# All twelve pieces of a layer's modulation weights inside the mixer; the first expert's weight loads unrolled ahead of the expert loop

## The chip, the cores and the metric

The kernel runs on one core of one Trainium2 chip. The metric is the device time of one execution in microseconds (us), as the median of several runs.

## What is computed

Two blocks follow each other, all in float32, on 256 tokens of 1024 features. The first block has two layers of a hybrid mixer and a mixture of 16 experts; the second block has two layers that are modulated by a condition. Cut to what matters here:

```python
# first block, for each of 2 layers
proj = rms_norm(h) @ w_in[layer]            # nine parts of 512 columns: rq rk rv rg hq hf_fwd hf_bwd hi hg
...                                         # retention scan and HGRN2 scan, both directions
h = h + concat([r_out, h_out]) @ w_out[layer]
affinity = softmax(rms_norm(h) @ w_router[layer])
gate, idx = top_k(affinity.T, 32)           # each expert chooses 32 tokens
hid = silu(xe @ w_gate[layer, e]) * (xe @ w_up[layer, e])
h = h.at[idx].add((hid @ w_down[layer, e]) * gate)

# second block, for each of 2 layers
sh1, sc1, gt1, sh2, sc2, gt2 = split(silu(cond) @ w_ada[layer] + b_ada[layer], 6)   # for c and c_ctx
...                                         # pool mixer or attention, MLP; both use the six modulations
```

The modulation product `silu(cond) @ w_ada[layer]` (1024 x 6144 weights for each layer) depends on nothing of the first block. The kernel computes it in twelve pieces of 512 columns per layer, beside the first block.

## The kernel before, in words

**The ring.** All large weights go through `ring`, six slots of 2 MB in SBUF. SyncE (SP) issues every load in one program order; before a load it waits until the item that had the slot before has been used. The counter for this is `weights_used`, which TensorE raises once per item, in the order in which it uses them. So a load that waits holds back all loads behind it. In the mixer only slots 0 to 3 carry items, in turn; the room of slots 4 and 5 holds `w_high`, the rounded copies of two items. An item of the mixer is therefore issued when the item four places before it has been used. `items` and `free_at` (lines 281 to 297) hold the slot, the number and the wait of each item.

**The mixer.** `mixer_items()` (line 79) is the order, written by hand, in which TensorE uses the items of a layer: nine projections (RQ, RK, HFF, HFB, HQ, RV, HI, RG, HG) and, between them, pieces of `w_ada` (ADA). Behind them come the two halves of `w_out`. ScalarE (`high_item`, line 1090), VectorE and GpSimd (`low_item`, line 400) split each projection item in two halves into a rounded part (`w_high`) and the rest (`w_low`), since a product is done as three passes of reduced precision (`product`, lines 461 to 463). The split items numbered 5 and more (RV, HI, RG, HG and the two of `w_out`) get their low part from GpSimd. Which rounded copy ScalarE makes when is tied to places in the item list: the copy of the item three places ahead (`n + 3 in SPLIT`), and `w_out` 0 one place before the last projection. It stands in ScalarE's program between the copies of ADA rows, and waits for the item's landing.

**An ADA piece** is on TensorE 8 products with `silu(c)` (line 473) into bank 6, then on ScalarE a copy of the bank to `ada_rows` (through line 376, a helper that records every turn), then on TensorE 4 small products that turn the rows to columns (line 482) into bank 7, then on VectorE the addition of the bias into `mods`. The columns of one piece are done just ahead of the next piece's products.

**Units.** Between the projections of RV, HI, RG and HG, TensorE runs 16 units of the HGRN scan (line 619, the last two line 612), two after each half of a projection. VectorE prepares each unit (`kdec`, `qdec`, `hgrn_x`, `hgrn_f`) and merges it. VectorE's order follows the same item list: the bias of the piece before at each ADA, four units at each projection.

**Before the change** six pieces stand in the mixer and six, called late, behind `w_out`: one ahead of the router (line 728), one behind its logits (line 740), four behind the turned affinities (line 748). `late_columns` gathers the columns of the late ones in one bank and VectorE adds their bias once. Two of the late pieces use slots 4 and 5. Then SP waits for the second `w_out` item and enters the expert loop (line 2181), with six items for each expert: four of gate and up weights, two of down weights, 12 MB together.

**The expert loop.** For each expert TensorE gathers 32 tokens (line 778), multiplies by gate and up (line 791), turns, multiplies by down (line 809), and scatters (line 819). The items of expert e + 1 are issued as those of expert e are used.

Of the kernel before, what the change touches and what calls it, by code (L numbers as in the profile page):

```python
# [22 lines left out]
ALU = mybir.AluOpType  # L23
# [8 lines left out]
P = 128  # L32
D = 1024
KC = D // P
# [64 lines left out]
def build_program(nc, x, cols, w_in, w_out, w_router, w_gate, w_up, w_down, final_g, ctx_x, w_ada,  # L99
# [184 lines left out]
    for layer in range(DEPTH):  # L284
# [3 lines left out]
        slots += [order[n % 6] for n in range(len(ADA_LATE) + 6 * NEXP)]  # L288
        names = ([("mix", layer, n) for n in range(len(mixer_items()))]
                 + [("w_out", layer, n) for n in range(2)]  # L290
                 + [("late", layer, n) for n in ADA_LATE]
                 + [("moe", layer, e, n) for e in range(NEXP) for n in range(6)])
# [52 lines left out]
    def freed(eng, name):  # L345

        eng.wait_ge(*read_by[name])
# [76 lines left out]
    def _(pe):  # L424
# [64 lines left out]
        for l in range(DEPTH):  # L489
# [198 lines left out]
            late_bank = [None]  # L688

            def late_ada(n):  # L690

                if n == ADA_LATE[0]:
                    ada_columns(l, n - 1, ("ada_c", l, n - 1))
                else:
                    late_columns(n - 1)
                ada_item(l, ("late", l, n), n, ("ada", l, n))

            def late_columns(n):
                name = ("ada_c", l, "late")
                freed(pe, ("ada", l, n))  # L700
                if n == ADA_LATE[0]:
                    late_bank[0] = take(pe, name, 7)
                for j in range(4):
                    at_ = 8 * (n - ADA_EARLY) + 2 * j
                    ins = mm(late_bank[0][:, at_:at_ + 2], ada_s[:, j * P:(j + 1) * P], K("sel"),
                             start=True, stop=True)
                if n == ADA_LATE[-1]:
                    fill(ins, name)


# [17 lines left out]
            late_ada(ADA_LATE[0])  # L728
# [11 lines left out]
            late_ada(ADA_LATE[1])  # L740
# [6 lines left out]
            for n in ADA_LATE[2:]:  # L747
                late_ada(n)
            late_columns(ADA_LATE[-1])
# [294 lines left out]
    def _(act):  # L1044
# [79 lines left out]
        for l in range(DEPTH):  # L1124
# [102 lines left out]
            def ada_row(n):  # L1227
                name = ("ada", l, n)
                ps = full(act, name)
                free(f(ada_s[:, :], ps[:, :], ACT.Copy), name)  # L1230

# [3 lines left out]
            ada_row(ADA_LATE[0])  # L1235
# [11 lines left out]
            for n in ADA_LATE[1:]:  # L1247
                ada_row(n)
# [191 lines left out]
    def _(dve):  # L1440
# [80 lines left out]
        for l in range(DEPTH):  # L1521
# [181 lines left out]
            ada_bias(ADA_EARLY - 1)  # L1703
# [25 lines left out]
            for i, what in enumerate((topf, top)):  # L1729
# [3 lines left out]
            name = ("ada_c", l, "late")  # L1733
            ps = full(dve, name)
            n = 4 * len(ADA_LATE)
            free(tt(mods[:, l, 4 * ADA_EARLY:4 * ADA_ALL, :],
                    ps[:, 0:2 * n].rearrange("p (a b) -> p a b", b=2),
                    C("b_ada", NMOD * KC * l + 4 * ADA_EARLY, n).unsqueeze(2)
                    .broadcast_to([P, n, 2]), ALU.add), name)
# [405 lines left out]
    def _(sp):  # L2145
# [20 lines left out]
        for l in range(DEPTH):  # L2166
# [10 lines left out]
            for n in ADA_LATE:  # L2177
                load(("late", l, n), chunked(w_ada[l, :, n * 512:(n + 1) * 512]), eight)

            sp.wait_ge(weights_used, items[("w_out", l, 1)][1] + 1)  # L2180
            with sp.Fori(0, NEXP) as e:
                for n in range(6):
                    slot, number, _ = items[("moe", l, 0, n)]
                    sp.wait_ge(weights_used, 6 * e + (number - RING1 + 1))
                    if n < 4:
                        dst = ring[:, slot, :].rearrange("p (k a f) -> p k a f", k=2, a=2)
                        for a, w in enumerate((w_gate, w_up)):
                            src = w[l, bass.ds(e, 1), 2 * n * P:2 * (n + 1) * P, :]
# [129 lines left out]
```

## Time and profile before

| | us |
|---|---|
| median of 3 runs | 2313.32 |
| lowest, highest of the 3 runs | 2312.31, 2318.74 |
| span of the profiled execution | 2314.5 |
| TensorE busy in it | 1928.7 (83%) |
| VectorE busy | 816.0 (35%) |
| ScalarE busy | 605.9 (26%) |
| GpSimd busy | 170.2 (7%) |

The page gives no time of the profiled execution beside its span of 2314.5 us, which lies 1.2 us above the median. The span runs from the first to the last instruction of the slowest core. Shares of busy time are averages over stages with different limits, so the stages are read apart: mixer of layer 0 (to about 243 us), its router and first expert, its experts (to about 759 us), the same three for layer 1 (to about 1518 us), and the second block.

### The profile page before, as it was taken

Reading aid. Unit: us, or ns where it says so; the run is one execution under the profiler, and the core shown is the slowest. Engines: PE = TensorE matmul, PEld = TensorE weight load, DVE = VectorE, ACT = ScalarE, POOL = GpSimd, SP = SyncE. Lnnn points to the kernel's source line nnn. Section 1 sums busy time; section 2 is a strip of 40 time slices with the busy share of each in tenths; the row PEclk is TensorE's granted clock in tenths of the full one; section 3 lists DMA queues with packets and bytes.
Section 4 is the critical chain, followed back from the end, with each engine's and each line's share of the span. In section 5 each row is a group of like instructions: output and inputs, shape, how many; then the busy total and the mean of one; then the engine's idle time right before and its main releaser. Section 6 shows DMA issues by size and latency. Waiting matters only on the chain.

```text
span 2314.5 us, 26791 instructions
## 1 busy us (share of the span) xinstructions
PE 1928.7 (83%) x10580; PEld 1227.7 (53%) x10580; DVE 816.0 (35%) x1196; ACT 605.9 (26%) x850; POOL 170.2 (7%) x70
## 2 busy tenths in 40 slices
PE   6897887777777789788767777766999999987998
PEld 5876532222232587654222222235888887445887
DVE  6566200000000556630000000046454455564776
ACT  5523211101111452312111111135222122253433
POOL 1333000000000132300000000021000000010000
PEclk9998887777777799888788888888999999998999
DMA  7373999999999636389999999941322224302551
GB/s 265 110 254 112 345 375 410 410 410 410 409 410 410 229 136 219 145 309 382 410 410 409 410 410 409 410 185 37 109 74 107 108 73 148 116 27 106 184 182 55
DMA packets 184534, 585.99 MB, mean 253 GB/s; under 512 B 6688, under 2 KB 7840, under 8 KB 184224
## 3 DMA queue, kind: packets, MB, share of 16 engines
q1 hardware_dynamic: 183152, 579.89, 65.0%
q0 software_dynamic: 896, 3.67, 0.4%
q10 hardware_dynamic: 432, 1.70, 0.2%
q8 instruction: 35, 0.57, 0.1%
q14 instruction: 19, 0.16, 0.0%
HBM read 584.19 MB, written 1.05 MB: 253 GB/s over the span
## 4 chain that ended last, share of the span: by engine, by line
PE 56%; DMA 17%; SPq 13%; DVE 7%; ACT 5%; issue 2%; POOL 1%; DVEq 0%; ACTq 0%; POOLq 0%
DMA ring<-in_w_down 16%; SPq L2189 11%; PE bank L461 10%; PE bank L463 10%; PE bank L462 10%; PE bank L791 3%; PE bank L778 3%; PE bank L809 3%; PE bank L819 3%; PE bank L940 2%; PE bank L619 2%; PE bank L473 2%; SPq L2195 2%; PE bank L1031 1%; ACT w_high L376 1%
## 5 line engine op out<-in xcount | busy, mean ns | idle before, releaser
L791 PE MATMUL bank<-ring,xeT 128*32 128x512 f32 x2048 | 280.9, 698 | 77.8 <-DMA ring<-in_w_up 58.7
L809 PE MATMUL bank<-ring,hid_T 128*32 128x512 f32 x1024 | 201.5, 930 | 81.2 <-DMA ring<-in_w_down 69.6
L791 PEld LDWEIGHTS bank<-ring,xeT 128*32 128x32 f32 x2048 | 69.3, 121 | 250.2 <-issue 160.5
L461 PE MATMUL bank<-x_high,w_high 128*128 128x512 f32 (+1 forms) x512 | 174.7, 341 | 17.0 <-DVE x_low L376 12.0
L376 POOL TENSOR_TENSOR w_low<-ring,w_high 128x2048 fp32r<-128x2048 f32 x26 | 120.7, 4643 | 821.6 <-ACT w_high L376 819.8
L463 PE MATMUL bank<-x_high,w_low 128*128 128x512 f32 (+1 forms) x512 | 175.4, 343 | 0.0
L462 PE MATMUL bank<-x_low,w_high 128*128 128x512 f32 (+1 forms) x512 | 173.7, 339 | 0.0
L1842 DVE TENSOR_TENSOR w_low<-ring,w_high 128x1024 fp32r<-128x1024 f32 x128 | 152.9, 1232 | 36.0 <-ACT w_high L1298 32.7
L1298 ACT ACTIVATE w_high<-ring 128x1024 fp32r<-128x1024 f32 x128 | 127.3, 1050 | 142.6 <-DMA ring<-in_w_mlp_in 64.0
L461 PE MATMUL bank<-w_high,hid_high 128*128 128x512 f32 x384 | 150.4, 392 | 0.0
L462 PE MATMUL bank<-w_low,hid_high 128*128 128x512 f32 x384 | 150.4, 392 | 0.0
L463 PE MATMUL bank<-w_high,hid_low 128*128 128x512 f32 x384 | 150.3, 391 | 0.0
L809 PEld LDWEIGHTS bank<-ring,hid_T 128*32 128x32 f32 x1024 | 35.1, 143 | 209.7 <-DMA ring<-in_w_down 135.9
L819 PE MATMUL bank<-y_e,gate_T 128*128 128x512 f32 x256 | 117.5, 601 | 29.1 <-DVE y_e L1779 29.1
L1776 DVE TENSOR_TENSOR hid_e<-silu_g,bank 128x256 f32<-128x256 f32 x32 | 13.5, 421 | 362.2 <-ACT silu_g L1255 362.2
L1779 DVE COPY y_e<-bank 128x512 f32<-128x512 f32 x32 | 22.1, 692 | 306.8 <-PE bank L809 306.8
L461 PE MATMUL bank<-w_high,xs_high 128*128 128x512 f32 x256 | 108.5, 424 | 18.8 <-DVE xT_low L376 15.5
L778 PEld LDWEIGHTS bank<-onehot,xs 128*128 128x128 f32 x1024 | 123.5, 201 | 0.0
L778 PE MATMUL bank<-onehot,xs 128*128 x1024 | 123.5, 281 | 0.0
L461 PEld LDWEIGHTS bank<-x_high,w_high 128*128 128x128 f32 x512 | 97.3, 190 | 29.2 <-issue 17.6
L1255 ACT ACTIVATE silu_g<-bank 128x256 f32<-128x256 f32 x32 | 12.3, 384 | 380.1 <-PE bank L791 380.1
L819 PEld LDWEIGHTS bank<-y_e,gate_T 128*128 128x128 f32 x256 | 46.0, 189 | 122.2 <-ACT y_e L1260 76.3
(229 smaller groups left out, 2925.1 us busy)
## 6 DMA issues: line engine op xcount, KB each, us to landing
ring<-in_w_gate SPq DMA_DIRECT2D x128, 1024.0 KB, 18.5
ring<-in_w_up SPq DMA_DIRECT2D x128, 1024.0 KB, 18.6
ring<-in_w_down SPq DMA_DIRECT2D x64, 2048.0 KB, 22.4
ring<-in_w_ada SPq DMA_DIRECT2D x24, 2048.0 KB, 8.2
ring<-in_w_in SPq DMA_DIRECT2D x18, 2048.0 KB, 10.0
ring<-in_w_mlp_in SPq DMA_DIRECT2D x16, 2048.0 KB, 8.6
ring<-in_w_mlp_out SPq DMA_DIRECT2D x16, 2048.0 KB, 7.7
ring<-in_w_out SPq DMA_DIRECT2D x4, 2048.0 KB, 9.2
```

What stands on the lines that cost most here:

```text
L376: self.ins, self.mine = op(*args, **kw), "none"
L461: mm(ps, lh, rh, start=first, stop=False, skip_group_check=True)
L462: mm(ps, lh, rl, start=False, stop=False, skip_group_check=True)
L463: return mm(ps, ll, rh, start=False, stop=last, skip_group_check=True)
L473: ins = mm(ps[32 * g:32 * g + 32, :], cT[:, 2 * g + k, :], w[:, 2 * g + k, :], start=k == 0, stop=k == 1)
L778: ins = mm(psum[7][:, c * CAP:(c + 1) * CAP], xs[:, t, c * P:(c + 1) * P], onehot[:, t, bass.ds(e * CAP, CAP)], start=t == 0, stop=t == NT ...
L791: ins = mm(psum[4][32 * g:32 * g + 32, :], xeT[:, 2 * n + k, :], w[:, k, :, 256 * g:256 * (g + 1)], start=n == 0 and k == 0, stop=n == 3 a ...
L809: ins = mm(psum[5 + half][32 * g:32 * g + 32, :], hidT[:, n, 32 * g:32 * g + 32], w[:, g, half * 512:(half + 1) * 512], start=n == 0, stop ...
L819: ins = mm(psum[2 * half + t][:, :], GT[:, t * P:(t + 1) * P], Y[:, half * 512:(half + 1) * 512], start=False, stop=False, skip_group_chec ...
L1298: raw(w_high[:, n % 2, quarter(q)], ring[:, slot, quarter(q)], ACT.Copy).then_inc(S_("w_high_ready"), 1)
L1842: nc.vector.tensor_tensor(w_low[:, slot, quarter(q)], ring[:, slot, quarter(q)], w_high[:, n % 2, quarter(q)].bitcast(F32), ALU.subtract). ...
L2189: sp.dma_start(dst[:, :, a, :], src.rearrange("o (k p) f -> p (o k) f", p=P)).then_inc(landed[slot], 16)
```

## The change

Twelve ADA pieces stand in `mixer_items()`; the late pieces and all that belongs to them go. The loads of the first expert's six items are issued by `load`, each with the wait for its own slot, ahead of a loop over the experts 1 to 15.

```diff
 def mixer_items():
-    return [RQ, RK, HFF, HFB, HQ, RV, ADA, HI, ADA, ADA, RG, ADA, ADA, HG, ADA]
-ADA_EARLY, ADA_ALL = mixer_items().count(ADA), 12
-ADA_LATE = range(ADA_EARLY, ADA_ALL)
+    return [RQ, RK, HFF, HFB, HQ, RV, ADA, ADA, HI, ADA, ADA, ADA, ADA, RG, ADA, ADA, ADA, ADA,
+            HG, ADA, ADA]
+ADA_ALL = mixer_items().count(ADA)
...
-        slots += [order[n % 6] for n in range(len(ADA_LATE) + 6 * NEXP)]
+        slots += [order[n % 6] for n in range(6 * NEXP)]
...
-            if name == ("late", layer, ADA_EARLY):
+            if name == ("moe", layer, 0, 0):
                 count[2][4:6] = [count[0]] * 2
...
-            late_ada(ADA_LATE[0])
+            ada_columns(l, pending[0], ("ada_c", l, pending.pop()))
             transposes(("x2", l), lambda t: xs[:, t, :], xs_ready)
...
-            late_ada(ADA_LATE[1])
             pe.wait_ge(S_("affinity_ready"), NT * (l + 1))
...
-            for n in ADA_LATE[2:]:
-                late_ada(n)
-            late_columns(ADA_LATE[-1])
...
-            ada_row(ADA_LATE[0])
...
-            for n in ADA_LATE[1:]:
-                ada_row(n)
...
-            ada_bias(ADA_EARLY - 1)
+            ada_bias(ADA_ALL - 1)
...
-            for n in ADA_LATE:
-                load(("late", l, n), chunked(w_ada[l, :, n * 512:(n + 1) * 512]), eight)
-            sp.wait_ge(weights_used, items[("w_out", l, 1)][1] + 1)
-            with sp.Fori(0, NEXP) as e:
+            for n in range(6):
+                load(("moe", l, 0, n), expert_sources(slice(0, 1), n), expert_view(n))
+            with sp.Fori(1, NEXP) as e:
```

ScalarE, in the mixer of layer 0, from the copies of HI's product on. `ada_rows` is the copy of a piece's rows, `w_high` the rounded copy of an item (two halves), `ret_gate` the product of RG. Before:

```order
L376 ACTIVATE hgrn_v<-bank 128x512 [waits bank_free0,weights_used]
L376 ACTIVATE w_high<-ring 128x2048 [waits bank_free1,landed2,weights_used]
L376 ACTIVATE w_high<-ring 128x2048 [waits mix_high_ready]
L376 ACTIVATE ada_rows<-bank 128x512 [waits mix_high_ready,weights_used]
L376 ACTIVATE ada_rows<-bank 128x512 [waits bank_free6,weights_used]
L376 ACTIVATE ret_gate<-bank 128x512 [waits bank_free6,bank_full2]
```

and now:

```order
L376 ACTIVATE hgrn_v<-bank 128x512 [waits bank_free0,weights_used]
L376 ACTIVATE ada_rows<-bank 128x512 [waits bank_free1,weights_used]
L376 ACTIVATE ada_rows<-bank 128x512 [waits bank_free6,weights_used]
L376 ACTIVATE w_high<-ring 128x2048 [waits bank_free6,landed1,weights_used]
L376 ACTIVATE w_high<-ring 128x2048 [waits mix_high_ready]
L376 ACTIVATE ada_rows<-bank 128x512 [waits mix_high_ready,weights_used]
L376 ACTIVATE ada_rows<-bank 128x512 [waits bank_free6,weights_used]
L376 ACTIVATE ret_gate<-bank 128x512 [waits bank_free6,bank_full2]
```

The rounded copy of RG stood ahead of both rows of its stretch; it now stands between the second and the third of four.

SyncE, the loads of layer 0. Before:

```order
L2155 DMA ring<-in_w_ada 128x8x512 [waits weights_used]
L2155 DMA ring<-in_w_in 128x8x512 [waits weights_used]
L2155 DMA ring<-in_w_ada 128x8x512 [waits weights_used] x2
L2155 DMA ring<-in_w_in 128x8x512 [waits weights_used]
L2155 DMA ring<-in_w_out 128x8x512 [waits weights_used] x2
L2155 DMA ring<-in_w_ada 128x8x512 [waits weights_used] x6
L2181 UNCONDITIONAL_BRANCH [waits weights_used]
```

and now:

```order
L2113 DMA ring<-in_w_ada 128x8x512 [waits weights_used] x4
L2113 DMA ring<-in_w_in 128x8x512 [waits weights_used]
L2113 DMA ring<-in_w_ada 128x8x512 [waits weights_used] x2
L2113 DMA ring<-in_w_out 128x8x512 [waits weights_used] x2
L2113 DMA ring<-in_w_gate 128x2x1024 [waits weights_used]
L2113 DMA ring<-in_w_up 128x2x1024
L2113 DMA ring<-in_w_down 128x4x1024 [waits weights_used] x2
```

Four pieces stand ahead of RG and four ahead of HG in the queue, where one or two stood; the six behind `w_out` are gone, and the first expert's loads follow `w_out`, each with its own wait.

TensorE, from the last products of `w_out` to the router and the spread of the chosen indices, one piece of the difference:

```order
 L482 MATMUL bank<-consts_sb,ada_rows 128x2 x4
-L473 MATMUL bank<-ring,silu_c 32x512 x8
 L437 MATMUL bank<-consts_sb,xs 128x128 x16
-L737 MATMUL bank<-router_sb,xT 128x16 x16
-L705 MATMUL bank<-consts_sb,ada_rows 128x2 x4
-L473 MATMUL bank<-ring,silu_c 32x512 x8
-L745 MATMUL bank<-consts_sb,affinity 16x128 x2
-L705 MATMUL bank<-consts_sb,ada_rows 128x2 x4
-L473 MATMUL bank<-ring,silu_c 32x512 x8
```

Nothing of the pieces but the columns of the last one is left on TensorE behind `w_out`; the other lines of this piece come back in the changed kernel under new line numbers, without L705 and L473 between them.

## Rows read from the trace of the kernel before

**Rows 1.** Busy time by stretch, all engines: us, busy of each, PEclk, DMA share, GB/s.
```profile
0.00:243.00 243.00, 199.91 (x1194) 169.52 (x1195) 144.33 (x163) 94.87 (x113) 66.89 (x25) 0.92 0.51 182
243.00:291.00 48.00, 39.30 (x245) 26.19 (x243) 16.25 (x44) 11.89 (x21) 0.00 (x0) 0.79 1.03 399
295.10:758.60 463.50, 360.01 (x2170) 135.02 (x2165) 26.46 (x61) 65.50 (x92) 0.00 (x0) 0.79 1.02 408
```
**Rows 2.** The chain that ended last, layer 0's experts, layer 1's last: start, us, what.
```profile
306.12 22.31 DMA ring<-in_w_down
...
1493.91 23.60 DMA ring<-in_w_down
```
**Rows 3.** Timeline of TensorE, mixer of layer 0: start, us, engine, line, operation.
```profile
139.83 1.92 PE L473 MATMUL bank<-ring,silu_c 128*32 128x512 f32 x16
142.47 1.05 PE L482 MATMUL bank<-consts_sb,ada_rows 128*128 128x2 f32 x8 [0.72 <-ACT ada_rows L376]
143.45 1.92 PE L473 MATMUL bank<-ring,silu_c 128*32 128x512 f32 x16
...
213.83 2.40 PE L437 MATMUL bank<-consts_sb,xs 128*128 128x128 f32 x10 [4.56 <-DVE mods L376]
...
242.88 0.95 PE L482 MATMUL bank<-consts_sb,ada_rows 128*128 128x2 f32 x8
```
**Rows 4.** SyncE, RG's load (issued at 120.6 us) and HG's (145.4), time to landing.
```profile
DMA to landing us min/median/max: 9.0/9.0/9.0
...
DMA to landing us min/median/max: 10.3/10.3/10.3
```
**Rows 5.** Timeline of ScalarE, mixer of layer 0.
```profile
136.28 3.85 ACT L376 ACTIVATE w_high<-ring 128x2048 fp32r<-128x2048 f32 x2
...
175.06 3.86 ACT L376 ACTIVATE w_high<-ring 128x2048 fp32r<-128x2048 f32 x2 [4.15 <-DMA ring<-in_w_out]
```
**Rows 6.** TensorE at the lower clock: its timeline, and one stretch (us, busy, PEclk, DMA, GB/s).
```profile
189.72 2.08 PE L612 MATMUL bank<-qdec,kdec 128*128 128x128 f32 x8 [4.47 <-DVE qdec L376]
...
256.20 1.85 PE L705 MATMUL bank<-consts_sb,ada_rows 128*128 128x2 f32 x8
257.98 3.32 PE L473 MATMUL bank<-ring,silu_c 128*32 128x512 f32 x16
...
190.00:194.00 4.00, 3.79 (x17) 0.50 0.63 241
```
**Rows 7.** Timeline of GpSimd, mixer of layer 0.
```profile
177.05 9.79 POOL L376 TENSOR_TENSOR w_low<-ring,w_high 128x2048 fp32r<-128x2048 f32 x2 [4.66 <-ACT w_high L376]
207.71 9.44 POOL L376 TENSOR_TENSOR w_low<-ring,w_high 128x2048 fp32r<-128x2048 f32 x2 [20.88 <-ACT w_high L376]
```
**Rows 8.** Timeline of VectorE, mixer of layer 0.
```profile
176.74 0.69 DVE L376 TENSOR_TENSOR qdec<-hgrn_q,hgrn_f 128x512 f32<-128x512 f32 x1
177.46 4.94 DVE L376 TENSOR_TENSOR hgrn_x<-hgrn_x,hgrn_f 128x512 f32<-128x512 f32 x1
...
208.45 4.33 DVE L376 TENSOR_TENSOR ret_gate<-ret_gate,ret_stat 128x512 f32<-128x512 f32 x1
...
217.06 1.49 DVE L376 TENSOR_TENSOR xT_low<-xT,xs_high 128x512 fp32r<-128x512 f32 x2
...
226.21 0.69 DVE L376 TENSOR_TENSOR h<-h,bank 128x512 f32<-128x512 f32 x1 [3.99 <-PE bank L463]
```
**Rows 9.** Timeline, TensorE and VectorE, router of layer 0 to the spread of the indices.
```profile
258.73 0.50 DVE L376 TENSOR_SCALAR affinity<-logit,router_stat 128x16 f32<-128x16 f32 x2
...
261.23 0.39 PE L745 MATMUL bank<-consts_sb,affinity 128*16 128x128 f32 x2
...
267.78 0.68 DVE L376 TENSOR_TENSOR spread<-top_index_f,consts_sb 16x512 f32<-16x512 f32 x1
...
278.39 1.98 PE L761 MATMUL bank<-spread,ones 16*128 16x512 f32 x4
...
281.22 1.41 DVE L376 TENSOR_TENSOR gated<-onehot,bank 128x512 f32<-128x512 f32 x2
```

More of the change, by code:

```diff
@@ L287, in build_program @@
         order = [order[(len(slots) + n) % 4] for n in range(4)] + [4, 5]
-        slots += [order[n % 6] for n in range(len(ADA_LATE) + 6 * NEXP)]
+        slots += [order[n % 6] for n in range(6 * NEXP)]
         names = ([("mix", layer, n) for n in range(len(mixer_items()))]
                  + [("w_out", layer, n) for n in range(2)]
-                 + [("late", layer, n) for n in ADA_LATE]
                  + [("moe", layer, e, n) for e in range(NEXP) for n in range(6)])
         for name, slot in zip(names, slots):
-            if name == ("late", layer, ADA_EARLY):
+            if name == ("moe", layer, 0, 0):
                 count[2][4:6] = [count[0]] * 2
@@ L686, in _ @@
                     hgrn_out()
[L688 to L708, printed above, removed]
             def mix_ready(t):
@@ L1225, in out_ready @@
                     freed(act, ("w_out", l, n, t))
[L1227 to L1230, printed above, removed]
             for t in range(NT):
@@ L1731, in _ @@
                    delta, ALU.mult).then_inc(S_("spread_ready"), 1)
[L1733 to L1739, printed above, removed]
             if l == DEPTH - 1:
@@ L2176, in _, with expert_sources, expert_view @@
                 load(("w_out", l, n), chunked(w_out[l, :, n * 512:(n + 1) * 512]), eight)
-            for n in ADA_LATE:
-                load(("late", l, n), chunked(w_ada[l, :, n * 512:(n + 1) * 512]), eight)
-            sp.wait_ge(weights_used, items[("w_out", l, 1)][1] + 1)
-            with sp.Fori(0, NEXP) as e:
+            def expert_sources(e, n):
+                if n < 4:
+                    return [w[l, e, 2 * n * P:2 * (n + 1) * P, :].rearrange(
+                        "o (k p) f -> p (o k) f", p=P) for w in (w_gate, w_up)]
+                return [w_down[l, e, :, :].rearrange("o (g two p) d -> two p (o g) d",
+                                                     two=2, p=P)[n - 4]]
+            def expert_view(n):
+                if n < 4:
+                    return lambda s_: [s_.rearrange("p (k a f) -> p k a f", k=2, a=2)[:, :, a, :]
+                                       for a in range(2)]
+                return four
+            for n in range(6):
+                load(("moe", l, 0, n), expert_sources(slice(0, 1), n), expert_view(n))
+            with sp.Fori(1, NEXP) as e:
                 for n in range(6):
@@ L2184, in _ @@
                     sp.wait_ge(weights_used, 6 * e + (number - RING1 + 1))
[L2185 to L2188, printed above, removed]
-                            sp.dma_start(dst[:, :, a, :],
-                                         src.rearrange("o (k p) f -> p (o k) f", p=P)).then_inc(
-                                landed[slot], 16)
-                    else:
-                        src = w_down[l, bass.ds(e, 1), :, :].rearrange(
-                            "o (g two p) d -> two p (o g) d", two=2, p=P)[n - 4]
-                        sp.dma_start(ring[:, slot, :].rearrange("p (g d) -> p g d", g=4),
-                                     src).then_inc(landed[slot], 16)
+                    for out_, src in zip(expert_view(n)(ring[:, slot, :]),
+                                         expert_sources(bass.ds(e, 1), n)):
+                        sp.dma_start(out_, src).then_inc(landed[slot], 16)
         for l in range(DEPTH):
```

1 line of the change is left out of this document (added).

## The prediction

> **What bounds the kernel now.** I first cut the span into stages, since the page's shares average over them. From 295.1 to 758.6 us the DMA engines are full, at 408 GB/s [rows 1]; the chain of waits says the same, with a wait for a down-projection load of 22 to 24 us in every expert [rows 2]. Fifteen experts of 12 MB (12.58 million bytes) are 188.7 MB, and 463.5 us at 408 GB/s carry 189.1 MB. So this stage is a stream of fixed length. It starts when TensorE uses the first item of expert 0, because only then does a slot come free for expert 1. Whatever lands earlier than that gains nothing; whatever delays that moment delays the end one for one. The same holds for layer 1, whose last expert ends on such a load too [rows 2]. The second block is untouched. The question is therefore only how much earlier or later TensorE reaches expert 0 in each layer.
>
> That path has two parts. In the mixer (0 to 243 us) TensorE is busy 199.91 of 243 us and the DMA engines 0.51 [rows 1], so the mixer has DMA to spare but little TensorE. Behind it, from 243 to 291 us, DMA is full (1.03) and TensorE is busy 39.3 of 48 us [rows 1], partly with the late pieces. It looks tempting to move work from the second to the first. But the pieces take TensorE time wherever they stand, and in the second stage a part of them lies beside VectorE's search for the best tokens.
>
> **The gain behind the mixer.** The affinities are ready at 258.73 + 0.50 = 259.2 us; TensorE turns them at 261.23, since it is still in a late piece [rows 9]. That is 2.0 us, and with 0.3 to 0.4 us from the piece ahead of the router 2.3. VectorE then writes the first spread tensor until 268.46 us (267.78 + 0.68), and TensorE reads it only at 278.39, behind four late pieces and their columns [rows 9]. After the change it starts at 268.46 - 2.3 = 266.2. Those two products take 1.98 us; TensorE will have idled before them, so I take the lower clock, at which the small columns took 1.85 for 1.05 us and the products of a piece 3.32 for 1.92 us [rows 3, 6]: about 4.0 us. The gated tensor, at 281.22 before [rows 9], then starts at 270.3: **10.9 us earlier**. Bounds: 9 us, if something of VectorE's comes between, and 12.2 us at the full clock. The missing bias addition of the late pieces costs nothing either way; it lay under the same wait.
>
> The unrolled loads of expert 0 count as **zero**. They are issued as their slots come free and all have landed some 20 us after the last of w_out is used (six items take 31 us at 408 GB/s, and four of them, 20 us, come after w_out), while TensorE needs about 37 us from there to expert 0. Before, too, they did not hold it up. If that cover were gone, the cost could be some 5 us; a gain is excluded, as only the use of the first item frees a slot.
>
> **The cost in the mixer, layer 0; layer 1 is the same.**
>
> *a. TensorE's time.* Two pieces back to back are 3.62 us apart (139.83 to 143.45): columns 1.05, products 1.92, and a wait for ScalarE's copy [rows 3]. Five of the six added pieces stand between projections, where TensorE is nearly always busy: one before HI, two before RG, two before HG. 5 x 3.62 = **18.1 us**.
>
> *b. RG arrives late.* An item is issued when the item four places before it has been used. For RG this was the piece before HI, so a whole projection with four units lay between; now it is the first of the four pieces just ahead of RG. This piece ends where the second of two ended before, at 143.45 + 1.92 = 145.4 us [rows 3]. RG is issued there. A weight load behind another landed after 9.0 or 10.3 us, in the bounds of 8 to 10.3 [rows 4]; I take 9.0, as the load before it is 6 us ahead: 154.4. ScalarE's two rounded halves take 3.85 us [rows 5]: 158.2. As the order shows, ScalarE's copy of the third piece's rows is queued behind them: 158.8. The fourth piece needs that copy at 142.47 + 3 x 3.62 = 153.3. TensorE waits **5.5 us**. ScalarE can be held like this: before w_out's copy it stood 4.15 us for a landing [rows 5]. After a gap of 4.47 us TensorE ran at 1.2 GHz, granted clock 0.50 [rows 6]; so the fourth piece costs 1.85 + 3.32 = 5.17 for 2.97 us, **2.2 us** more. GpSimd's low halves (9.3 to 9.8 us [rows 7]) then just end in time. Together 7.7 us; bounds 4.5 (landing in 8 us, full clock) and 13 (10.3 us, and RG's first 24 products at the lower clock too).
>
> The Trainium skill, "DMA: Bandwidth & Descriptors", sections Specifications and Bandwidth, gives 0.6 us to the first byte and 425 GB/s for a large transfer, which would be an estimated 5.5 us for 2 MB. By that the wait would be 3.5 us shorter, twice in a layer, and the kernel's time 14 us less. The trace has 9.0 us for the same thing, and the trace decides.
>
> *c. HG arrives late*, by the same distances: **7.7 us**.
>
> *d. The last units.* VectorE operations with both inputs in SBUF take 0.69 us, but 4.94 while GpSimd makes its two low halves in 9.79 us [rows 7, 8]: such an operation waits for the end of a half, about 4.9 us. The wait is moved later with w_out 0, by about as much as the units are; I take -1 us, bounds -3 and +4.
>
> *e. The last piece* stands behind the scans, where TensorE idles. Its columns need the bank that VectorE frees with the bias of the piece before, queued behind VectorE's last write of xs (213.5 us). This write comes 3.6 us sooner, as GpSimd no longer works beside it (4.33 against 0.69 us [rows 8]): columns from 210.1, piece ended 215.3 at the lower clock, then all 16 transposes, 218.0. Before, they ended at 213.83 + 2.40 = 216.2 [rows 3]: **+1.8 us**.
>
> *f. w_out 1 is split late.* ScalarE makes its rounded copy after the rows of the last piece: 215.9 to 219.8, with ScalarE's own share of the xT chunks behind it. GpSimd's low halves then run from 217.9 to about 227.3, under VectorE's `xT_low`, which has two SBUF inputs and ran freely before (1.49 us for two, as GpSimd ended at 217.15 [rows 7, 8]). The first waits until 223.3, the second until 227.9, the third and fourth follow 2.1 us of chunks, at 230.7 and 231.4. The first w_out product, cut into four pieces by this and at the lower clock, ends at 235.9 instead of 226.2 [rows 8]: 9.7 us, of which 1.8 are in e. **+7.9 us**. Bounds: 0 if VectorE isn't held, 10.
>
> Sum: 18.1 + 7.7 + 7.7 - 1 + 1.8 + 7.9 = 42.2 us later at 242.88 us [rows 3], and 10.9 us back: **31.3 us for a layer, 62.6 for two**. The sum is made against the span of 2314.5; the median is 1.2 lower, and I take it as the base: 2313.3 + 62.6 = **2376 us**. With the bounds a layer loses 16 us (no lock, no clock lost) to 41 us: 2345 to 2395.
>
> **The rivals.**
>
> *The arrivals are covered.* The pieces cost only TensorE's time: 18.1 + 1.8 - 10.9 = 9 us a layer, **2331 us**. For it: ScalarE and DMA are slack on average. Against: the four-place distance, which the order shows.
>
> *The lower clock spreads.* With gaps of 5 us ahead of RG and HG the first 24 products of both go at 1.2 GHz (each about 4.6 us more), and landings take 10.3 us: 31.3 + 9.2 + 2.6 = 43 us a layer, **2400 us**.
>
> *Faster.* The mixer has DMA to spare, and gaps of TensorE for all six pieces. Then only the gain stays: 10.9, and the 3.6 us of VectorE in e, for a layer, **2284 us**. It decides for faster once the mixer grows by less than 10.9 us, that is if fewer than three of the five pieces show. For it: the mixer's gaps come to 43 us in sum [rows 1]. Against: between RV's and HG's projections TensorE hardly has any. The Trainium skill, same page, section Rules for kernel authors, asks to issue a DMA early and wait late, so that its cost overlaps; by that rule this case would come out. Here the loads move early, but so does their use, and RG and HG are issued later relative to theirs.
>
> *No change.* The change might not act, as its unrolled loads do not; or costs and gain cancel. Only the first case needs no luck, and the order shows that the pieces did move.
>
> **How the numbers follow.** Forecast 2376 us (its own range 2345 to 2395) 0.69; covered arrivals 0.11; spread clock 0.12; faster 0.04; no change 0.04. A time of this kernel can be told from no change at about 0.3%, 7 us. The range that holds 8 in 10 takes in the forecast's range and the covered arrivals, and leaves out most of the rest: 2328 to 2395. Slower 0.92, same 0.04, faster 0.04.
>
> **What would show it.** TensorE's gap ahead of the fourth piece before RG and before HG, of 4 to 6 us, released by ScalarE's `ada_rows`, and on ScalarE a wait for `in_w_in` of 5 us just before; `xT_low` of 4 us and more in the w_out stage; the spread product 2 us after the top-k chain; the expert stream again of 463 us from its start. Expert 0 reached less than 9 us later than before would make the forecast wrong; so would a stream that is shorter.

## The result, and the profile after

| | before | after |
|---|---|---|
| median, us | 2314.53 (4 runs, 2312.31 to 2318.74) | 2379.24 (4 runs, 2376.43 to 2382.62) |
| ratio, 95% interval | | 1.0281, 1.0262 to 1.0299 |
| span of the profiled execution | 2314.5 | 2380.8 |

The change makes the kernel 64.7 us slower; 2376 us was predicted (+62.6). I go through the profile after it at the places of the prediction's steps. The profiled execution of the change is the slowest of its four (2382.62 us), 3.4 us above the median, so a difference between two traces can be a few us off the difference of the medians. Times in this trace lie 0.7 us late from about 30 us on, where the two programs still do the same work: a difference between the two executions.

TensorE's timeline in the mixer of layer 0, after, with the pieces ahead of HI, RG and HG, the last units' end, and the last columns, at the end of `w_out`:

```profile
122.19 1.92 PE L473 MATMUL bank<-ring,silu_c 128*32 128x512 f32 x16
...
154.29 1.92 PE L473 MATMUL bank<-ring,silu_c 128*32 128x512 f32 x16
161.73 1.87 PE L482 MATMUL bank<-consts_sb,ada_rows 128*128 128x2 f32 x8 [5.51 <-ACT ada_rows L376]
163.53 3.45 PE L473 MATMUL bank<-ring,silu_c 128*32 128x512 f32 x16
166.91 0.50 PE L461 MATMUL bank<-w_high,xs_high 128*128 128x512 f32 x1
...
193.52 1.93 PE L473 MATMUL bank<-ring,silu_c 128*32 128x512 f32 x16
200.67 1.78 PE L482 MATMUL bank<-consts_sb,ada_rows 128*128 128x2 f32 x8 [5.22 <-ACT ada_rows L376]
202.38 3.64 PE L473 MATMUL bank<-ring,silu_c 128*32 128x512 f32 x16
...
228.53 5.16 PE L634 MATMUL bank<-ret_v,ret_scores 128*128 128x128 f32 x32
...
286.22 0.95 PE L482 MATMUL bank<-consts_sb,ada_rows 128*128 128x2 f32 x8
```

The gap ahead of the fourth piece is there twice, 5.51 and 5.22 us, each released by ScalarE's copy `ada_rows`, and the piece behind it runs at the lower clock (3.45 and 3.64 us for 1.92 [rows 3]). ScalarE's timeline shows why the copy is late:

```profile
157.14 3.85 ACT L376 ACTIVATE w_high<-ring 128x2048 fp32r<-128x2048 f32 x2 [3.88 <-DMA ring<-in_w_in]
161.08 0.60 ACT L376 ACTIVATE ada_rows<-bank 128x512 f32<-128x512 f32 x1
...
196.07 3.85 ACT L376 ACTIVATE w_high<-ring 128x2048 fp32r<-128x2048 f32 x2 [3.59 <-DMA ring<-in_w_in]
...
251.52 3.85 ACT L376 ACTIVATE w_high<-ring 128x2048 fp32r<-128x2048 f32 x2
```

It stands 3.88 us for RG's landing, makes two rounded halves, and only then copies the third piece's rows. Loads of projections have come into the chain of waits, which had none of them in a mixer before but the very first:

```profile
86.23 7.76 DMA ring<-in_w_in
...
149.03 8.04 DMA ring<-in_w_in
...
188.26 7.75 DMA ring<-in_w_in
```

The second is RG, issued at 149.03 us, the third HG. The first is **HI**, which no step of the prediction has: with a piece more ahead of it, it too waits for a later use (HQ's, where it was HFB's). Its rounded copy stands ahead of ScalarE's `hgrn_diag`, for which VectorE's `qdec` waits 7.23 us (1.83 before; but there `qdec` itself took 5.11 us beside GpSimd, and here 1.59, so less is lost than the wait shows).

VectorE's timeline in the same mixer, and under it GpSimd's row beside the `xT_low`:

```profile
99.55 1.59 DVE L376 TENSOR_TENSOR qdec<-hgrn_q,hgrn_f 128x512 f32<-128x512 f32 x1 [7.23 <-ACT hgrn_diag L376]
...
215.84 5.09 DVE L376 TENSOR_TENSOR qdec<-hgrn_q,hgrn_f 128x512 f32<-128x512 f32 x1
...
221.82 4.05 DVE L376 TENSOR_TENSOR kdec<-hgrn_k,hgrn_x 128x512 f32<-128x512 f32 x1
...
254.72 8.79 DVE L376 TENSOR_TENSOR xT_low<-xT,xs_high 128x512 fp32r<-128x512 f32 x2
...
269.55 0.69 DVE L376 TENSOR_TENSOR h<-h,bank 128x512 f32<-128x512 f32 x1 [2.37 <-PE bank L463]
```
```profile
253.51 9.46 POOL L376 TENSOR_TENSOR w_low<-ring,w_high 128x2048 fp32r<-128x2048 f32 x2 [28.19 <-ACT w_high L376]
```

Two `xT_low` take 8.79 us beside GpSimd's halves; they took 1.49 before [rows 8]. Behind `w_out`, TensorE's router stage after:

```profile
289.98 2.39 PE L437 MATMUL bank<-consts_sb,xs 128*128 128x128 f32 x10 [0.88 <-DVE mods L376]
294.25 6.98 PE L714 MATMUL bank<-router_sb,xT 128*128 128x16 f32 x32 [1.88 <-ACT xT L376]
304.16 0.60 PE L721 MATMUL bank<-consts_sb,affinity 128*16 128x128 f32 x2 [2.92 <-DVE affinity L376]
...
311.65 3.77 PE L734 MATMUL bank<-spread,ones 16*128 16x512 f32 x4 [5.19 <-DVE spread L376]
...
318.11 6.87 PE L751 MATMUL bank<-onehot,xs 128*128 x32
```

And busy time by stretch, columns as in [rows 1]: a part of the router stage, and the experts of layer 0.

```profile
290.00:301.00 11.00, 9.12 (x42) 8.75 (x42) 1.93 (x4) 1.90 (x4) 0.00 (x0) 0.50 1.02 414
329.00:793.00 464.00, 314.61 (x2174) 127.77 (x2170) 26.46 (x61) 65.49 (x92) 0.00 (x0) 0.95 1.02 408
```

The expert stream is as long and as full as it was (408 GB/s, DMA 1.02). It starts later, and that is the loss: the first gather stands at 318.11 us, 34.3 us later than before, when it was at 283.81. In layer 1 the gather moves a further 30.3 us: its last columns come 39.8 us later, less what layer 0 handed on, and 9.5 us come back behind them. The remaining 1.7 us between the two spans lie behind that gather.

**The account of layer 0.** Before, two pieces stood ahead of RG and two ahead of HG (the item lists show it; "one or two", further up, is wrong), 3.62 us apart [rows 3]. `ret_scores` is TensorE's product right behind the last two units. The columns "predicted" and "measured" are in us, later is positive.

| step | predicted | measured | from the rows |
|---|---|---|---|
| HI late | none | 2.9 | first products 122.19, before 118.61; less 0.7 |
| a. five pieces | 18.1 | 18.1 | spacing 3.62 again |
| b. RG late | 7.7 | 7.2 | 163.53 - 154.29 - 3.62, and 3.45 - 1.92 |
| c. HG late | 7.7 | 7.7 | 202.38 - 193.52 - 3.62, 1.72, and 0.7 in HG's first products |
| d. last units | -1 | -1.9 | what is left at `ret_scores`: 228.53, before 193.87 |
| e, f. last piece, late split | 9.7 | 8.7 | what is left at 286.22, before 242.88 [rows 3] |
| sum at the end of `w_out` | 42.2 | 42.6 | 286.22 - 242.88 - 0.7 |
| back behind it | -10.9 | -9.0 | 318.11 - 286.22 = 31.9, before 40.9 |
| layer | 31.3 | 33.6 | |

Within e and f, step e puts the end of the transposes back by 2.4 us (predicted 1.8), and the late split costs 6.3 us (predicted 7.9).

### The profile page after: what moved, and what is told of

It is laid out like the page before. It is cut to its first block, busy times and chain, and to the rows that moved or that the text cites. A ratio compares the mean times of both kernels' runs of the same rounds, so it can differ in the third digit from the quotient of the medians.

```text
span 2380.8 us, 26775 instructions
## 1 busy us (share of the span) xinstructions
PE 1905.5 (80%) x10580; PEld 1231.8 (52%) x10580; DVE 819.9 (34%) x1206; ACT 606.0 (25%) x850; POOL 170.1 (7%) x70
## 4 chain that ended last, share of the span: by engine, by line
PE 55%; DMA 18%; SPq 14%; DVE 7%; ACT 3%; issue 2%; POOL 1%; DVEq 0%; ACTq 0%; POOLq 0%
DMA ring<-in_w_down 16%; SPq L2158 14%; PE bank L461 11%; PE bank L463 11%; PE bank L462 11%; PE bank L751 3%; DMA ring<-in_w_in 3%; PE bank L792 3%; PE bank L913 2%; PE bank L764 2%; PE bank L619 2%; PE bank L782 2%; PE bank L473 2%; PE bank L1004 1%; ACT w_high L376 1%
## 5 line engine op out<-in xcount | busy, mean ns | idle before, releaser
L764 PE MATMUL bank<-ring,xeT 128*32 128x512 f32 x2048 | 272.2, 674 | 112.0 <-DMA ring<-in_w_up 92.9
L782 PE MATMUL bank<-ring,hid_T 128*32 128x512 f32 x1024 | 161.5, 764 | 91.1 <-DMA ring<-in_w_down 88.9
L782 PEld LDWEIGHTS bank<-ring,hid_T 128*32 128x32 f32 x1024 | 31.9, 127 | 200.6 <-DMA ring<-in_w_down 143.2
L462 PE MATMUL bank<-w_low,xs_high 128*128 128x512 f32 x256 | 106.0, 414 | 0.0
```

The lines of the kernel that those rows point to most:

```text
L462: mm(ps, lh, rl, start=False, stop=False, skip_group_check=True)
L764: ins = mm(psum[4][32 * g:32 * g + 32, :], xeT[:, 2 * n + k, :], w[:, k, :, 256 * g:256 * (g + 1)], start=n == 0 and k == 0, stop=n == 3 a ...
L782: ins = mm(psum[5 + half][32 * g:32 * g + 32, :], hidT[:, n, 32 * g:32 * g + 32], w[:, g, half * 512:(half + 1) * 512], start=n == 0, stop ...
```

## The experiments

My theory is the prediction's: of a mixer's 42 us, TensorE's own time is some 20, the late arrivals of RG and HG 15, and the turn of `w_out` 1's split 8. The rivals: the pieces alone cost the time; the arrivals cost through GpSimd and not through ScalarE's queue; or the unrolled loads matter.

**x1_loop**: the change, with the first expert's loads back in the loop.

```diff
-            for n in range(6):
-                load(("moe", l, 0, n), expert_sources(slice(0, 1), n), expert_view(n))
-            with sp.Fori(1, NEXP) as e:
+            sp.wait_ge(weights_used, items[("w_out", l, 1)][1] + 1)
+            with sp.Fori(0, NEXP) as e:
```

> The changed kernel, with expert 0's loads put back into the expert loop behind one wait for the second w_out item. Theory: the unrolled loads are worth nothing, since expert 1's stream starts when TensorE uses the first item of expert 0, and in the changed kernel that is 38 us after w_out, while six items need 31 us: 2379 us, within 4. Rival: loading expert 0 early gives something back; then this kernel is slower by up to 5 us a layer, 2389.

Measured 2377.86 us (2374.08 to 2386.61), ratio 1.0292 (1.0264 to 1.0319): no difference from the change (1.0281). The unrolled loads are worth nothing, as predicted; the whole loss belongs to the pieces.

**x2_six**: the change, with the item order of before, so six pieces and none late.

```diff
-    return [RQ, RK, HFF, HFB, HQ, RV, ADA, ADA, HI, ADA, ADA, ADA, ADA, RG, ADA, ADA, ADA, ADA,
-            HG, ADA, ADA]
+    return [RQ, RK, HFF, HFB, HQ, RV, ADA, HI, ADA, ADA, RG, ADA, ADA, HG, ADA]
...
+        tick(memset(mods[:, :, 4 * ADA_ALL:, :], 0.0))
```

> Only the six pieces that the mixer had before; the other six are left out altogether (their modulations are zero, so the second block computes with other numbers). Theory: this is the kernel before without its late pieces, and shows the gain behind the mixer by itself: 9 to 11 us a layer off the kernel before, 2293 to 2297 us. The changed kernel then pays 82 to 86 us in the mixers. Rival: the late pieces were hidden beside the search for the best tokens: within 4 us of the kernel before, 2314.

Measured 2295.09 us (2292.24 to 2295.36), ratio 0.9917 (0.9901 to 0.9934). The late pieces are worth 17.6 us behind the mixers, 8.8 a layer (by its trace, from the last columns to the gather, 9.6 and 10.1); the same six pieces cost 2379.2 - 2295.1 = 84 us inside them. As in the change, the router's products take 6.98 us here.

**x3_twice**: all twelve pieces' products, but each of the six items is used for two pieces, so that the item order and all loads of the mixer are those of before.

```diff
-    return [RQ, RK, HFF, HFB, HQ, RV, ADA, ADA, HI, ADA, ADA, ADA, ADA, RG, ADA, ADA, ADA, ADA,
-            HG, ADA, ADA]
+    return [RQ, RK, HFF, HFB, HQ, RV, ADA, HI, ADA, ADA, RG, ADA, ADA, HG, ADA]
...
-ADA_ALL = mixer_items().count(ADA)
+ADA_ALL = 2 * mixer_items().count(ADA)
...
-                    ada_item(l, ("mix", l, n), ada_n[0], ("ada", l, ada_n[0]))
+                    for twice in range(2):
+                        ada_item(l, ("mix", l, n), ada_n[0], ("ada", l, ada_n[0]), twice == 1)
```

> Twelve pieces in the mixer, but in the item order of the kernel before: each of the six ADA items is used for two pieces, one right after the other (so half of the modulations come from the wrong weights, and six loads a layer are left out). TensorE, ScalarE and VectorE do all twelve pieces; only the distances in the ring are as before. Theory: the late arrivals are gone (2.9 us at HI, 7.1 at RG, 7.1 at HG in each layer), the time of the pieces stays: 2379 - 34 = 2345 us. Rival (all the cost is TensorE's time for the pieces): 2379. Rival (it is nearly all arrival): under 2325.

Measured 2337.57 us (2336.39 to 2338.74), ratio 1.0103 (1.0086 to 1.0120). TensorE's and ScalarE's timelines at the fourth piece before RG, in x3_twice (its lines are one or two off):

```profile
154.48 1.05 PE L484 MATMUL bank<-consts_sb,ada_rows 128*128 128x2 f32 x8 [0.72 <-ACT ada_rows L375]
```
```profile
141.05 3.85 ACT L375 ACTIVATE w_high<-ring 128x2048 fp32r<-128x2048 f32 x2
...
190.31 3.87 ACT L375 ACTIVATE w_high<-ring 128x2048 fp32r<-128x2048 f32 x2
...
210.77 0.60 ACT L375 ACTIVATE square<-bank 128x512 f32<-128x512 f32 x1 [1.19 <-PE bank L636]
```

With the item it needs there in time, ScalarE makes RG's copy without a wait, and TensorE's gap is the usual 0.72 us instead of 5.51. So 2379.2 - 2337.6 = 41.7 us of the 64.7 come from arrivals (the six loads fewer that a layer has here are part of that). I had counted 8 us less: `w_out` 0 lands in time too, its copy starts at 190.31 without a wait, where it has one of 7.10 us in the change, and GpSimd's halves no longer fall on the last units. They still hold two of VectorE's operations (5.08 and 4.94 us), but those of earlier units, for which TensorE waits only 0.46 us. From the fourth piece's copy (189.56) to the first `square` (210.77) pass 21.2 us here, 25.9 in the change (206.09 to 231.94).

**x5_copy_first**: the change, with the rounded copy of `w_out` 1 ahead of the last rows' copies.

```diff
                       scale=1.0 / P).then_inc(S_("ret_std_ready"), 1)
+                    high_item(l, SPLITS - 1)
...
-            high_item(l, SPLITS - 1)
             high_chunks(("mix", l), mix_gain)
```

> The changed kernel, with ScalarE's rounded copy of the second w_out item ahead of the row copies of the last two pieces. Theory: GpSimd's low halves come 11 us sooner and no longer hold VectorE's xT_low (8.8 us for two), but hold its ret_gate again (3.6 us), which delays the bias that the last piece waits for: 2 to 3 us a layer, 2374 us. Rival (the lock on xT_low counts in full): 8 us a layer, 2363. Rival (it is the last piece itself, not the lock): no change, 2379.

Measured 2373.47 us (2372.72 to 2374.71), ratio 1.0260 (1.0243 to 1.0278). GpSimd and VectorE, layer 0, in x5_copy_first:

```profile
240.65 9.88 POOL L376 TENSOR_TENSOR w_low<-ring,w_high 128x2048 fp32r<-128x2048 f32 x2 [15.36 <-ACT w_high L376]
```
```profile
256.41 1.49 DVE L376 TENSOR_TENSOR xT_low<-xT,xs_high 128x512 fp32r<-128x512 f32 x2
...
263.94 0.69 DVE L376 TENSOR_TENSOR h<-h,bank 128x512 f32<-128x512 f32 x1 [2.37 <-PE bank L463]
```

GpSimd has ended before `xT_low`, which takes 1.49 us again, and the first `h` comes 5.6 us earlier. Its `xT_low` starts 1.7 us later than in the change, as `ret_gate` waits for GpSimd again (4.08 us), so between the two places 7.3 us are gained: step f is confirmed here. By the traces the gather comes 5.6 us earlier in layer 0 and 3.2 in layer 1; the medians differ by 5.8 us in all, which is the 2 to 3 us a layer that I expected.

**x4_rows_first**: the change, with the rounded copies of RG and HG behind all four rows' copies, so that no row waits for a landing.

```diff
-                if n > 5 and n + 3 in SPLIT:
-                    high_item(l, SPLIT.index(n + 3))
+                if n > 5 and n + 1 in SPLIT and n + 1 > 8:
+                    high_item(l, SPLIT.index(n + 1))
```

> The changed kernel, with ScalarE's rounded copies of RG and HG behind the row copies of all four pieces before them. Theory: the wait only moves. The third piece's rows are copied at once and the fourth piece is done 5 us sooner, but the product then waits for the low halves, which come 7 us and 12 us after a landing that is where it was: 1.5 to 2 us less for each of RG and HG, 2379 - 7 = 2372 us. Rival (the place in ScalarE's queue is the cause, not the landing): 7 us for each, 2351.

Measured 2388.73 us (2385.67 to 2391.09), ratio 1.0328 (1.0312 to 1.0343): slower than the change by 9.5 us, where I expected 7 us less. TensorE and ScalarE in x4_rows_first:

```profile
158.34 1.92 PE L473 MATMUL bank<-ring,silu_c 128*32 128x512 f32 x16
167.68 0.77 PE L461 MATMUL bank<-w_high,xs_high 128*128 128x512 f32 x1 [7.42 <-POOL w_low L376]
```
```profile
160.33 0.60 ACT L376 ACTIVATE ada_rows<-bank 128x512 f32<-128x512 f32 x1 [3.03 <-PE bank L473]
161.04 3.85 ACT L376 ACTIVATE w_high<-ring 128x2048 fp32r<-128x2048 f32 x2
```

The gap ahead of the fourth piece is gone: it was ScalarE's queue. But RG's copy now waits for the fourth row (160.33), not for the landing, and ends 4 us later; TensorE then stands 7.42 us for GpSimd's first half, which needs the copy. I had counted the copy and the low halves from the landing, and left out that the copy, behind the fourth row, starts only after it. Both places in the queue cost, once the item is late; the cause is the lateness. The two traces hold only 4.4 us of the 9.5: the gather stands 1.1 us later than in the change in layer 0 and 4.4 us later in layer 1.

**x6_hi**: the change, with HI one piece earlier, so that it waits for HFB again.

```diff
-    return [RQ, RK, HFF, HFB, HQ, RV, ADA, ADA, HI, ADA, ADA, ADA, ADA, RG, ADA, ADA, ADA, ADA,
+    return [RQ, RK, HFF, HFB, HQ, RV, ADA, HI, ADA, ADA, ADA, ADA, ADA, RG, ADA, ADA, ADA, ADA,
```

> The changed kernel with one piece moved from ahead of HI to behind it, so that HI's load waits for the item it waited for before. Theory: HI's late arrival, 2.9 us on VectorE's first unit in layer 0 of the changed kernel's trace, goes in both layers, and RG's wait stays, as it is still issued at the second piece behind HI: 2373 us. Rival (the 2.9 us is covered by something else a little later): 2379. Rival (five pieces in a row make RG's wait longer): 2380 or more.

Measured 2383.54 us (2382.20 to 2386.10), ratio 1.0305 (1.0289 to 1.0321). TensorE and ScalarE in x6_hi:

```profile
119.07 1.92 PE L473 MATMUL bank<-ring,silu_c 128*32 128x512 f32 x16
...
161.42 1.87 PE L482 MATMUL bank<-consts_sb,ada_rows 128*128 128x2 f32 x8 [8.33 <-ACT ada_rows L376]
```
```profile
156.83 3.85 ACT L376 ACTIVATE w_high<-ring 128x2048 fp32r<-128x2048 f32 x2 [6.70 <-DMA ring<-in_w_in]
```

HI's lateness is gone (119.07 for 122.19), which shows it to be the 2.9 us. But the columns behind RG's late copy stand at 161.42, 0.3 us from where they were: RG was issued at 145.9, 3.6 us behind the load ahead of it (6.2 in the change), and landed only at 156.8, 10.9 us later. The 3 us went into a longer wait, as the last rival said; the gather of both layers stands within 0.3 us of the change's. The median is 4.3 us above the change's, with overlapping intervals, and no row shows these 4.3 us.

**z1_wout0**: the kernel before, with the rounded copy of `w_out` 0 moved behind the last units. In the kernel before it starts GpSimd's halves under those units [rows 7, 8].

```diff
-                if n == SPLIT[-1] - 1:
-                    high_item(l, SPLITS - 2)
                 if kind == HG:
+                    high_item(l, SPLITS - 2)
```

> The kernel before, with ScalarE's rounded copy of the first w_out item behind the copies of the last two units instead of ahead of HG's. GpSimd's low halves then run while VectorE waits for the scans' outputs. Theory (VectorE's operations with two SBUF inputs wait for a running GpSimd operation): the two locked operations of 4.94 and 4.95 us take 0.69 each, TensorE's gap of 4.4 us before the last two units goes, and these run at the full clock: 5 to 6.5 us a layer, 2313 - 11 = 2302 us. Rival (the low halves now hold something else, or the w_out product waits for them): no gain, 2313 or more.

Measured 2293.15 us (2291.67 to 2298.02), ratio 0.9907 (0.9892 to 0.9923): 22 us faster, twice what I expected. TensorE, VectorE and GpSimd in z1_wout0:

```profile
184.49 1.95 PE L612 MATMUL bank<-qdec,kdec 128*128 128x128 f32 x16
...
240.23 4.53 PE L737 MATMUL bank<-router_sb,xT 128*128 128x16 f32 x32 [2.02 <-ACT xT L376]
```
```profile
182.15 0.69 DVE L376 TENSOR_TENSOR qdec<-hgrn_q,hgrn_f 128x512 f32<-128x512 f32 x1
...
216.48 0.69 DVE L376 TENSOR_TENSOR h<-h,bank 128x512 f32<-128x512 f32 x1 [2.87 <-PE bank L463]
```
```profile
189.17 9.24 POOL L376 TENSOR_TENSOR w_low<-ring,w_high 128x2048 fp32r<-128x2048 f32 x2 [17.38 <-ACT w_high L376]
```

The last units run together from 184.49 us, where the first stood behind a gap at 189.72 and at the lower clock [rows 6]; the first `h` comes at 216.48 for 226.21 [rows 8], and the router's 32 products take 4.53 us for 6.39. Lock and clock together bring layer 0's gather 11.3 us forward (272.46 for 283.81), of which 0.6 us were there before the place of the move, and layer 1's by a further 13.7. The mixer's reserve was here, not in where the pieces stand.

**z3_after**: the change with the same move.

```diff
-                if n == SPLIT[-1] - 1:
-                    high_item(l, SPLITS - 2)
                 if kind == HG:
+                    high_item(l, SPLITS - 2)
```

> The changed kernel with the move of z1_wout0. Theory: the same lock on VectorE (5.09 and 4.05 us) goes, and HG's output copy no longer waits behind the late w_out load on ScalarE: 5 us a layer, 2369 us. Rival (in the changed kernel this wait is set by the late w_out load itself): 2376 or more.

Measured 2370.16 us (2364.97 to 2373.02), ratio 1.0227 (1.0207 to 1.0248): 9 us under the change. The last units run together here too (from 221.99 us), and `ret_scores` starts at 223.78 for 228.53, but the gather of layer 0 gains only 3.6 us and that of layer 1 a further 5.9. The two operations held before the move were about as long as in the kernel before (5.09 and 4.05 us against 4.94 and 4.95); `w_out` 1's halves still hold `xT_low` (9.05 us). Why the gain is less than half of z1_wout0's was not tried.

**y1_spread**: the kernel before, with the spread and one-hot tensors made ahead of its last two late pieces, instead of behind all.

```diff
-            for n in ADA_LATE[2:]:
+            for n in ADA_LATE[2:4]:
                 late_ada(n)
-            late_columns(ADA_LATE[-1])
...
+            for n in ADA_LATE[4:]:
+                late_ada(n)
+            late_columns(ADA_LATE[-1])
```

> The kernel before, with the spread of the indices (and VectorE's one-hot tensors) ahead of its last two late pieces instead of behind them; twelve pieces, six of them late. Theory: behind w_out TensorE's time is the bound; two waits for ScalarE of 0.72 us and the 3 us in which it waited for the one-hot and gated tensors are filled with pieces: 2 to 3 us a layer, 2308 us. Rival (expert 0's last loads, issued as the pieces are used, come later and hold the first expert): no gain or up to 5 us slower. Rival: within 3 us of before.

Measured 2311.59 us (2307.02 to 2320.74, 11 runs), ratio 0.9995 (0.9983 to 1.0006): no difference. The spread products do run at 270.63 for 278.39 [rows 9]. VectorE in y1_spread:

```profile
280.93 0.21 DVE L376 TENSOR_TENSOR mods<-bank,cols_sb 128x48 f32<-128x48 f32 x1 [6.06 <-PE bank L705]
281.27 0.29 DVE L1771 COPY gate_sel<-gated 128x256 f32 x1
```

The late bias stands ahead of `gate_sel` in VectorE's queue and waits there for the last columns. From the end of `w_out` to the gather it is 37.6 us for 40.7 in layer 0, and 39.8 for 41.1 in layer 1, where `mod_gain` stands there as well: of 8 us, 3 and 1 reach the gather, and the runs don't show even those.

**y2_both**: y1_spread with the first piece ahead of RV.

```diff
-    return [RQ, RK, HFF, HFB, HQ, RV, ADA, HI, ADA, ADA, RG, ADA, ADA, HG, ADA]
+    return [RQ, RK, HFF, HFB, HQ, ADA, RV, HI, ADA, ADA, RG, ADA, ADA, HG, ADA]
```

> As y1_spread, and the first piece of the mixer moved ahead of RV, into the 6 us in which TensorE waits for VectorE's first units; the ring's distances for HI, RG and HG stay. Theory: another 1.9 us a layer, 2304 us, 0.4% under the kernel before. Rival: RV is issued one item later and its split is late, which takes it back: as y1_spread or slower.

Measured 2309.59 us (2307.15 to 2312.77, 11 runs), ratio 0.9984 (0.9975 to 0.9993): smaller than expected, and within the 0.3% that I named as what can be told from no change.

**z2_all**: y2_both with the move of z1_wout0, and `mod_gain` behind the expert loop.

```diff
-                if n == SPLIT[-1] - 1:
-                    high_item(l, SPLITS - 2)
                 if kind == HG:
+                    high_item(l, SPLITS - 2)
...
                 nc.vector.tensor_copy(Y[:, 512:D], psum[6][:, :]).then_inc(S_("y_right_ready"), 1)
+            if l == DEPTH - 1:
...
+                            tick(stt(mod_gain[:, l2, which, s, :],
```

> y2_both with the same move as z1_wout0, and with the eight small mod_gain operations of the last layer behind the expert loop instead of ahead of expert 0. Theory: the gains add, as they lie in different stages: 2310 - 11 - 2 = 2297 us, 0.7% under the kernel before. Rival: less than 2305 is not reached, since the pieces behind w_out are bound by their loads.

Measured 2290.02 us (2289.44 to 2290.23), ratio 0.9888 (0.9872 to 0.9903). It is 1.1% under the kernel before, but not clearly better than z1_wout0: the medians are 3 us apart, the intervals overlap, and the gathers of the two traces stand within 0.6 us of each other in both layers (273.08 for 272.46, 1016.64 for 1016.76). That the gains add is not shown.

## Why the prediction was right

**The frame held.** The stream is fixed, and only the moment of the first gather counts: 34.3 and 30.3 us of the 66.3 between the spans stand there.

**The arrivals held.** Steps b and c were mechanism and size right: a distance of four items, a landing, two halves on ScalarE, a row's copy behind them, and TensorE stands. RG was issued at 149.0 us (145.4 predicted; HI's 2.9 and the trace's 0.7 on top). It landed in 8.0 us where I took 9.0, so TensorE stood 4.8 us beyond the usual 0.72, for the 5.5 of the prediction. x3_twice takes the arrivals away and takes 41.7 of 64.7 us with them. The Trainium skill, "DMA: Bandwidth & Descriptors", Specifications and Bandwidth, by which 2 MB would be there in an estimated 5.5 us, is too short for each of these loads: 7.75 and 8.04 us in the chain. Its rule to issue early and wait late (same page, Rules for kernel authors) found no case here: loads issued earlier gave nothing (x1_loop), and what counted was the distance from one item's use to the next item's use.

**The rival of covered arrivals (2331 us) falls**, and x3_twice at 2337.6 comes near its number where they are covered (its `xT_low` still waits, 8.34 us, which the rival left out). The lower clock did not spread over RG's and HG's products: three of HG's took it, none to speak of RG's. Faster and no change fall with the result.

**One term was missing: HI late, 2.9 us.** I looked at RG and HG, for which the distance shrank most, and not at HI, which got a piece more ahead of it too. x6_hi shows it.

**One term was too large: the gain behind the mixer**, 10.9 us against 9.0 (and 8.8 in x2_six). The spread product ran as predicted (3.77 us against 4.0). The step that failed is the first, "2.0 us, and with 0.3 to 0.4 us from the piece ahead of the router 2.3": the affinities are turned 17.9 us behind the last columns (304.16 - 286.22), and before it was 18.35, so 0.4 came of 2.3. With the piece ahead of the router gone, ten transposes wait for a bias (`mods`, 0.88 us) and TensorE idles; its granted clock is 0.50 from 290 to 301 us, and the router's products take 6.98 us for 6.39, so that the affinities are ready 1.5 us later behind the last columns than before (17.9 us for 16.4). It is tempting to say that the work which I moved away had kept the clock up. That is not shown: before, with the piece in place, the clock fell in the router's products too, and in x4_rows_first, with the piece gone, these are no longer than before. Before, and in x4_rows_first:

```profile
249.97 6.39 PE L737 MATMUL bank<-router_sb,xT 128*128 128x16 f32 x32 [2.02 <-ACT xT L376]
```
```profile
296.11 6.24 PE L714 MATMUL bank<-router_sb,xT 128*128 128x16 f32 x32 [2.29 <-ACT xT L376]
```

The granted clock over these products is 0.55 and 0.57.

**The other terms were a little too large**: e and f 8.7 for 9.7, b 7.2 for 7.7, and d 0.9 better. In layer 0, HI's 2.9 and the 1.9 of the gain go one way, these 2.4 the other, which leaves 2.3 us too little (33.6 against 31.3). In layer 1 the forecast was 1.0 us too much: 39.8 us at the last columns for 42.2, and 9.5 back for 10.9. Of the 3.2 us between 2376 and 2379.24, 1.2 are the base, since the kernel before is at 2314.53 here and at 2313.32 there. That the total came out so close is in part luck: errors of 2 to 3 us in single terms have cancelled.

## What to carry to other kernels

In a ring whose loads wait in program order for an earlier item's use, an inserted item costs its own time and one place of lead for every item behind it: count, for each load, what lies between the use that frees its slot and its own use, and compare with a landing. If a conversion in another engine's in-order queue needs the item, look up what stands behind the conversion, and who reads it. Before moving work between stages, look for elementwise GpSimd work under a chain of two-input VectorE operations: one moved copy gave 22 us here, where moving six pieces lost 65.

## What the runs showed of the hardware that I had not expected

**The same short products took 4.5 to 7 us.** The 32 products of the router took 4.53 us in z1_wout0 at a granted clock of 0.80, 6.39 before at 0.55, and 6.98 in the change at 0.50, which is 1.2 GHz. The order of work just ahead of them is the same in z1_wout0 and before, so this order alone doesn't set it; what does was not tried.

**Half a microsecond decides over nearly five.** Layer 1's last unit in the change and in x1_loop, whose compute programs are the same. GpSimd and VectorE in the change:

```profile
1005.63 9.54 POOL L376 TENSOR_TENSOR w_low<-ring,w_high 128x2048 fp32r<-128x2048 f32 x2 [9.85 <-ACT w_high L376]
```
```profile
1005.97 4.85 DVE L376 TENSOR_TENSOR kdec<-hgrn_k,hgrn_x 128x512 f32<-128x512 f32 x1
1010.85 4.87 DVE L376 TENSOR_TENSOR qdec<-hgrn_q,hgrn_f 128x512 f32<-128x512 f32 x1
```

and in x1_loop:

```profile
1007.25 9.84 POOL L376 TENSOR_TENSOR w_low<-ring,w_high 128x2048 fp32r<-128x2048 f32 x2 [9.89 <-ACT w_high L376]
```
```profile
1007.00 0.69 DVE L376 TENSOR_TENSOR kdec<-hgrn_k,hgrn_x 128x512 f32<-128x512 f32 x1
1007.73 4.97 DVE L376 TENSOR_TENSOR qdec<-hgrn_q,hgrn_f 128x512 f32<-128x512 f32 x1
```

Where `kdec` starts 0.3 us behind GpSimd it waits out a half, and `qdec` the next; where it starts 0.25 us ahead, only `qdec` waits. `ret_scores` follows at 1016.95 and at 1013.76, although x1_loop was 1.6 us late until then: 4.8 us from such a meeting (the lower clock on the unit behind the gap included). It may be what spreads x1_loop's runs from 2374 to 2387 us; that was not tried. The Trainium skill, "SBUF — State Buffer", section "SBUF: two separate sides", says that whichever of a two-input VectorE operation and a GpSimd operation starts first has the shared ports for its whole length; these rows agree, 0.69 us against 4.85.

**2 MB landed in 7.75 to 10.9 us.** From issue to landing, the loads of HI, RG and HG took 7.76, 8.04 and 7.75 us in the change. The load ahead of RG's and HG's had been issued 6.2 us earlier. RG's and HG's took 9.0 and 10.3 before [rows 4], 5.4 and 3.6 us behind the load ahead, and RG's 10.9 in x6_hi, 3.6 us behind it. A load close ahead goes with a late landing in these five, but it is not all: HI's took 9.2 us before and 7.76 in the change, both 12.4 us behind the load ahead. What sets the time was not measured by itself.
